# Gated linear attention and the merge in one software-pipelined loop, with the silu gate made in the projection

## The reference, cut to what matters

```python
def _gla_chunk(S, inp):            # o_t = q_t S_t, S_t = diag(alpha_t) S_{t-1} + k_t^T v_t
    b = jnp.cumsum(g, axis=1)
    o_inter = jnp.einsum('blhk,bhkv->blhv', qf * jnp.exp(b), S)
    A = jnp.einsum('bthk,bshk,btshk->bhts', qf, kf, decay)       # decay = exp(b_t - b_s), s <= t
    o_intra = jnp.einsum('bhts,bshv->bthv', A, vf)
    S_new = jnp.exp(b_last)[..., None] * S + jnp.einsum('blhk,blhv->bhkv', k_dec, vf)

def _merge(fox_o, gla_o, gr, gla_norm_g, w_out):
    gn = gla_o * lax.rsqrt(jnp.mean(jnp.square(gla_o), axis=-1, keepdims=True) + EPS)
    gated = gn.reshape(B, T, GLA_VW) * gla_norm_g * jax.nn.silu(gr)
    return jnp.concatenate([fox_o, gated], axis=-1) @ w_out
# x = x + merge; h = rmsnorm(x) * norm2_g; then the FFN on h
```

## Time and profile before

| | |
|---|---|
| median of three runs | 3477.89 us |
| the profiled execution | 3477.98 us, span 3476.2 us |
| PE busy over the span | 3133.6 us (90%) |
| DVE / ACT / POOL busy | 2027.8 / 1207.3 / 556.0 us |
| stretch of `gla` and `merge` up to the first FFN matmul | 1300.4 to 1898.4, 598.0 us |

### The profile page before, as it was taken

The page is one execution under the profiler, slowest core; times in us unless marked ns, Lnnn a source line. Parts: engine busy times, 40 slices in busy tenths (PEclk is TensorE's granted clock), DMA queues, the critical chain, the costliest instruction groups (busy, mean ns, idle before and its releaser), DMA issues. The chain is left out here.

```text
span 3476.2 us, 50599 instructions
## 1 busy us (share of the span) xinstructions
PE 3133.6 (90%) x19097; PEld 2887.6 (83%) x19097; DVE 2027.8 (58%) x3535; ACT 1207.3 (35%) x2345; POOL 556.0 (16%) x388
## 2 busy tenths in 40 slices
PE   7999999789999584665996999999999899999996
PEld 5899999768777363554775999999999899999996
DVE  5232211179999347993442666666666666666665
ACT  6352111168888224552221222222223422222223
POOL 0010000000000004650000222121222322122122
PEclk9999999889999795777998999999999999999998
DMA  4245322352431522223556211111114321111112
GB/s 119 71 150 174 129 74 56 79 104 64 90 67 32 144 119 64 79 74 114 165 165 226 71 49 42 48 45 45 48 42 162 108 79 43 48 48 42 48 33 77
DMA packets 247867, 298.79 MB, mean 86 GB/s; under 512 B 35785, under 2 KB 205062, under 8 KB 238680
## 3 DMA queue, kind: packets, MB, share of 16 engines
q1 hardware_dynamic: 245136, 289.88, 28.4%
q10 hardware_dynamic: 1344, 4.36, 0.6%
q0 software_dynamic: 1264, 2.88, 0.3%
HBM read 204.85 MB, written 92.21 MB: 85 GB/s over the span
## 5 line engine op out<-in xcount | busy, mean ns | idle before, releaser
L2290 PE MATMUL ps_ffn<-h,wsp_n 128*128 128x312 f32 (+1 forms) x6336 | 1051.8, 322 | 22.0 <-DMA h<-h2T 22.0
L2290 PEld LDWEIGHTS ps_ffn<-h,wsp_n 128*128 128x128 f32 x6336 | 1012.3, 188 | 27.1 <-issue 22.3
L2216 DVE TENSOR_TENSOR yacc<-ps_ffn,yacc 128x312 f32<-128x312 f32 (+1 forms) x1008 | 488.0, 519 | 388.3 <-PE ps_ffn L2308 388.3
L629 PE MATMUL ps_project<-hT,wsp 128*128 128x416 f32 (+1 forms) x3000 | 600.7, 356 | 0.0
L629 PEld LDWEIGHTS ps_project<-hT,wsp 128*128 128x128 f32 (+1 forms) x3000 | 546.2, 185 | 23.9 <-issue 8.7
L2308 PE MATMUL ps_ffn<-aT,dsp 128*128 128x312 f32 (+1 forms) x3168 | 547.3, 322 | 3.0 <-DVE yacc L2216 2.9
L2308 PEld LDWEIGHTS ps_ffn<-aT,dsp 128*128 128x128 f32 x3168 | 508.3, 188 | 6.6 <-DVE yacc L2216 3.5
L2192 ACT ACTIVATE aT<-a 128x416 fp32r<-128x416 f32 x132 | 65.1, 493 | 820.5 <-DVE a L2267 820.5
L2095 POOL TENSOR_TENSOR wsp_n<-wraw_n,wsp_n 128x1024 fp32r<-128x1024 f32 x88 | 210.7, 2396 | 814.8 <-ACT wsp_n L2136 814.8
L2258 DVE RECIPROCAL silu<-silu 128x416 f32<-128x416 f32 x132 | 304.9, 2310 | 28.7 <-ACT silu L2181 28.6
L485 DVE COPY zr<-ps_project 104x512 f32<-104x512 f32 x80 | 55.2, 692 | 300.6 <-PE ps_project L641 175.6
(11 more groups left out here) (261 smaller groups left out, 3544.4 us busy)
## 6 DMA issues: line engine op xcount, KB each, us to landing
wraw_n<-in_w_gate_dram SPq DMA_DIRECT2D x44, 512.0 KB, 3.8
wraw_n<-in_w_up_dram SPq DMA_DIRECT2D x44, 512.0 KB, 3.8
draw<-in_w_down_dram SPq DMA_DIRECT2D x44, 512.0 KB, 3.6
h2T<-hT_m SPq DMA_DIRECT2D x20, 832.0 KB
h<-h2T SPq DMA_DIRECT2D x20, 832.0 KB, 13.8
zT<-zs SPq DMA_DIRECT2D x12, 1040.0 KB, 4.0
wraw<-in_w_in_dram SPq DMA_DIRECT2D x24, 512.0 KB
x<-x2s SPq DMA_DIRECT2D x20, 416.0 KB
```

The costliest lines, as they stand in the source:

```text
L629: last = pe.matmul(ps[0:w, p % NB, 0:BLK], wsp[:, b, s, k, 0:w], hT[:, g * TPB:(g + 1) * TPB, v, k, :], start=k == 0 and m == 0, stop=k == ...
L2216: dve.tensor_tensor(y, z, y, ALU.add).then_inc(added, 1)
L2290: last = pe.matmul(ps[:, 2 * q + s, 0:FB[b] * TT], wsp[:, par, s, w, k, :], h2[:, FB0[b]:FB0[b + 1], v, k, :], start=m == 0, stop=m == 3 * ...
```

## The change

`gla` and `merge` become one stage `gla_merge` with a loop of steps t = 0 ... 18 over 17 chunks (chunk 0 is the 32 sample tokens, chunks 1 to 16 have 128 prompt tokens). Step t holds the scores, outputs and state of chunk t, the turning, splitting and output product of chunk t-1, and the turning of the normalised rows of chunk t-2. GLA outputs stay on chip; `mixg` and `gsq` are gone. `w_out` is loaded through a double buffer at the stage's start. The diagonal of the scores is now an elementwise product on POOL (`dq`) summed by one-column matmuls. `h2T` is laid out over all tokens instead of by tile. The gate is made in `project`, for the last four column tiles: ACT Exp and +1, DVE reciprocal and a product with the block and the norm weight.

```diff
 # project, ACT, in place of the copy L382 for n >= 21
+                if n >= N_GATE:
+                    m = p - place(N_GATE, 0)
...
+                    act.activation(silu, ps[:, p % NB, 0:BLK], ACT.Exp, scale=-1.0).then_inc(s_exp, 1)
+                    act.wait_ge(s_exp, m + 1)
+                    act.activation(silu, silu, ACT.Identity, bias=ones[:]).then_inc(s_one, 1)
+                    return
 # project, DVE
+            def gate_rows(p):
+                n, g = BLOCKS[p]
...
+                dve.wait_ge(s_one, m + 1)
+                dve.reciprocal(silu, silu).then_inc(s_inv, 1)
...
+                dve.scalar_tensor_tensor(out=zs[:, n % 2, g * BLK:(g + 1) * BLK], in0=ps[:, p % NB, 0:BLK], scalar=gn[:, n - N_GATE:n - N_GATE + 1],
+                                         in1=silu, op0=ALU.mult, op1=ALU.mult).then_inc(block_out, 1)
...
+                if N_GATE <= n < NWT:
+                    gate_rows(p)
 # gla_merge, ACT
+            for t in range(NCH + 2):
+                if is_gla(t - 1):
+                    high_m(t - 1, 0)
+                if t + 1 < NCH:
+                    exps(t + 1)
...
+                if is_gla(t):
+                    key_rows(t)
+                if t >= 2:
+                    high_h(t - 2, 0)
+                if is_gla(t - 1):
+                    high_m(t - 1, 1)
+                if t >= 2:
+                    high_h(t - 2, 1)
+                if is_gla(t):
+                    squares(t)
+                if is_gla(t - 1):
+                    square_x(t - 1)
+                if t <= NCH:
+                    roots(t)
+                if is_gla(t):
+                    scale_o(t)
 # gla_merge, DVE, the loop's body for a full step
+                    low_m(t - 1, 0)
...
+                        pick(t, i)
+                        if i == 0 and t >= 2:
+                            low_h(t - 2, 0)
+                        if i == 1 and t >= 1:
+                            low_m(t - 1, 1)
+                        if i == 5 and t >= 2:
+                            low_h(t - 2, 1)
+                    pick_diagonal(t)
...
+                    add(t - 1, 0)
...
+                    decayed(t + 1)
...
+                    add(t - 1, 1)
...
+                    update(t)
...
+                    exponents(t + 2)
...
+                    invert(t)
...
+                    norm(t - 1)
...
+                    gate(t)
 # layout of the normalised rows for the FFN
-    "x2": ((NTOK, D), F32), "h2T": ((NT, P, 2, KD, TT), F32),
+    "x2": ((NTOK, D), F32), "h2T": ((P, 2, KD, NTOK), F32),
```

More of the change, by code:

```diff
@@ L1510, in _ @@
         @block.tensor
         def _(pe):
-            pe.wait_ge(filled, 3 + 2 * NL)
-            pe.wait_ge(zeroed, 4)
-            def back(t, b, L):
-                pe.wait_ge(k_ready, t + 2)
-                pe.wait_ge(q_ready, t + 2)
-                if not isinstance(t, int) or t >= 0:
-                    pe.wait_ge(picked, (t + 1))
-                    pe.wait_ge(kd_out, t + 1)
-                for l, half in levels(L):
+            pe.wait_ge(filled, 4 + 2 * NL)
+            pe.wait_ge(zeroed, 6)
@@ L1522, in back, with scores @@
+            def scores(c):
+                b, L = c % 2, width(c)
+                pe.wait_ge(k_ready, c + 1)
+                pe.wait_ge(q_ready, c + 1)
+                if c:
+                    pe.wait_ge(picked, c)
+                if c >= 2:
+                    pe.wait_ge(added, 2 * (c - 1))
+                for l, half in levels(c):
                     for g in range(2):
@@ new lines, in _ @@
+            lows, highs = range(4), range(4, KD)
+            for t in range(NCH + 2):
+                if is_gla(t - 1):
+                    turn_mix(t - 1, 0)
+                if is_gla(t):
+                    scores(t)
+                if t >= 2:
+                    turn_h(t - 2, 0)
+                if is_gla(t - 1):
+                    turn_mix(t - 1, 1)
+                    products(t - 1, 0, lows)
+                if t >= 2:
+                    turn_h(t - 2, 1)
+                if is_gla(t - 1):
+                    products(t - 1, 0, highs)
+                if is_gla(t):
+                    outputs(t)
+                if is_gla(t - 1):
+                    products(t - 1, 1, lows)
+                    products(t - 1, 1, highs)
+                if is_gla(t):
+                    state(t)
@@ new lines, in gate @@
+            def gate(c):
+                b, L = c % 2, width(c)
+                dve.wait_ge(o_out, c + 1)
+                dve.wait_ge(v_come[b], 32 * (c // 2 + 1))
+                if c >= 2:
+                    dve.wait_ge(m_turned, 2 * (c - 1))
+                dve.tensor_tensor(mix[0:L, b, FOX:D], ov[0:L], sg[0:L, b], ALU.mult).then_inc(gated, 1)
+            exponents(0)
+            decayed(0)
+            for k in range(4):
+                low_w(k)
+            dve.wait_ge(st_in, 16)
@@ L2364, in stream_step @@
     fox_sample(nc, d)
-    gla(nc, d)
-    merge(nc, d)
+    gla_merge(nc, d)
     ffn(nc, d)
```

843 lines of the change are left out of this document (431 added, 412 removed).

## The result

The changed kernel takes 3361.26 us (median of 4 runs, 3358.64 to 3361.88) against 3478.44 for the kernel before beside it: a ratio of 0.9662, with 0.9645 to 0.9679 as the 95% interval. The forecast was 3374, the range 3345 to 3425. The profiled execution took 3358.64 us with a span of 3356.9.

A forecast was written before the change was run, and what follows sets the result against it. DVE bounded `gla` and TensorE `merge`, taking turns. Merged: 39.6 + 375 + 20.6 + 18.7 + 6.3 + 23.5 = 483.7 against 598.0 us; 3478.0 - 114.3 + 10 for the gate = 3373.7, say 3374 us, range 3345 to 3425.

The forecast's parts named there:

- What sets the step: Merged loop: ACT's queue from 0.7 to 11.35 us, DVE's picks to 17.1, then TensorE's last 7.6.
- The length of the step: Merged loop: a full step takes 25.0 us, fifteen of them 375 us.
- the walk: Merged loop: one full step followed instruction by instruction over the engines with estimated handoffs, giving 24.7 us.
- The ends: Merged stage outside the fifteen full steps: 39.6 us start, then 20.6, 18.7, 6.3 and 23.5 us.
- T = 0: Point where TensorE ends a product and DVE can add it; first full step's put 39.6 us after stage start.
- the last turn: End of merged stage: add, squares, root, norm, two turns with a split between, 6.3 us.
- the way to the FFN: From the merged stage's last turn to the FFN's first matmul: old 22.0 us plus 1.5 for h2T's layout, 23.5.
- The gate: In project: 2 us at each of three tile borders and 4 at the end, 10 us more; bounds 4 and 25.
- (2): Merged loop: ACT's queue longer through handoffs or dearer table switches, 2.8 us a step, 42 in all, 3416 us; chance 0.18.
- (3): Merged loop: TensorE binds and a step falls to 22 us, 45 us less, 3329 us; chance 0.08.
- (5): Layout change or gate costs more than set, at the bounds 6 and 25 us together, 3394 us; chance 0.17.
- (4): Merged loop: TensorE's clock falls after gaps ahead of the outputs, 7.3 us a step, 110 in all, 3484 us; chance 0.04.

The follow-up runs named there:

- e3_exps_late: Changed kernel with ScalarE's exponentials of the next chunk moved behind the high halves of the norm and of h: 3343.17 us, ratio 0.9613.
- e5_no_root: Changed kernel with the square root in the merged loop left out, so no table loads there: 3344.86 us, ratio 0.9624.
- e2_rows_first: Changed kernel with VectorE in project taking the earlier block's rows out of PSUM ahead of the newest block's gate: 3360.14 us.
- f4_late_filler_tanh: Changed kernel with exponentials behind the high halves, five unused TensorE products per full step, and project's gate made from tanh without the reciprocal: 3316.73 us, ratio 0.9538.
- f2_late_filler: Changed kernel with ScalarE's exponentials behind the high halves and five unused TensorE products added per full step: 3330.45 us.
- e8_gap: Changed kernel with seven added VectorE products ahead of each step's last pick, so TensorE stands still before the outputs: 3474.71 us.
- f1_filler_alone: Changed kernel with only five unused TensorE products added per full step, behind the scores: 3363.42 us.
- e4_invert_first: Changed kernel with VectorE's reciprocal of the roots ahead of its exponent sums: 3369.83 us, ratio 0.9688.
- e1_gate_only: Kernel before the change with only the gate moved into project, old gated attention and merge kept: 3481.8 us, ratio 1.0008.

## Why the prediction was right, point by point

**What sets the step: right.** The waits named ahead are there: VectorE 2.98 us for ScalarE's high half of h (38.7 us in 13 steps), 2.37 for TensorE ahead of the second add, TensorE 0.97 ahead of the outputs. `e3_exps_late` and `e5_no_root` show that ScalarE's queue sets it: taking the exponentials out from ahead of the high halves, or the second table load out of the queue, shortens the step. The clock in the loop is 0.97, over the 0.95 that was named.

**The length of the step: right in kind, too long by 1.4.** Predicted 25.0 (24.7 by the walk and 0.3 put on top), measured 23.58. Against the walk the high half of h ends at 10.5 instead of 10.75, the last pick at 16.2 instead of 17.1, and TensorE's last stretch takes 7.4 instead of 7.6. Of the 1.1 us of the walk, 0.25 are on ScalarE, 0.65 on VectorE between the high half and the last pick, 0.2 on TensorE. The walk added lengths where the instructions overlap: on ScalarE the exponential of 0.42 starts at 1548.58 and the next one 0.33 later, and that one, of 1.90, is followed at 1550.71, 1.80 later (rows of the step above). The Trainium skill ("ScalarE: Activation LUTs", What ACT_TABLE_LOAD costs) says that back-to-back activations overlap by some 93 ns; the trace agrees with 0.09 to 0.10. On VectorE the ten splits and picks from 1551.59 to 1557.25 have lengths that sum to 6.0 us and take 5.66, and the walk had 6.3 for them; four of the picks take 0.44 us and not the 0.52 of the earlier trace rows. TensorE's waits come out shorter too: in a step at full clock (1517.52 to 1541.09) 3.0 us in five waits of at most 1.0, not about 5 in five of at most 1.6. So this term of the sum was mis-sized, 15 x 1.4 = 21 us: nothing should have been put on top, and starts should have been subtracted, not lengths added.

**The ends: right in the sum, within 1.3 us each.** T = 0 came 38.3 us after the stage's start (39.6 predicted); the sixteenth step took 20.8 (20.6), the seventeenth 19.1 (18.7), the last turn 7.5 (6.3), the way to the FFN 23.0 (23.5). That these errors cancel (-1.3 + 0.2 + 0.4 + 1.2 - 0.5 = 0.0) is luck. The 322 GB/s that the prediction names there stand as 317 in the earlier trace rows; its 1.5 us hang little on it.

**The gate: right place, 4.4 us too cheap.** 14.4 instead of 10, with TensorE's waits at the tile borders and at the end, as said. Within it the shares were off: the copies that open a tile cost 5.5 us of waits and 1.5 of clock instead of 6, the end 7.0 instead of 4. What I missed is that the chain (4.76 us) is nearly as long as a block with its turn (5.00), so that what it loses at a border is still there when the matmuls end, and the last turns wait for it in full; `e2_rows_first` showed it by failing and `f4_late_filler_tanh` by removing the 2.75.

**The rivals.** (2) did not come: no dearer switch. (3), TensorE binding, came only once the exponentials were moved, and then at 21.33 us, not 22 (`f2_late_filler`). (5) did not come either: the gate stayed under its bound of 25, and the way to the FFN took 23.0 us, less than the term. (4) was priced at 7.3 us a step for a full fall; a real fall ahead of the outputs costs 2.3 (`e8_gap`), since the clock is back by 1531.5 and most of the product runs at the upper level. And it does not need a gap of 5 us: behind the scores the clock falls with single waits of 0.40 and 0.76 us. The Trainium skill ("TensorE: Matmul & The Clock Gate", HAM oscillation) draws such a loop with long waits for transfers; here the trace shows falls where no single wait is longer than 0.8. In the changed kernel they cost nothing only because ScalarE was later still (`f1_filler_alone`).

**The sum.** 3373.7 - 21.1 (stage) + 4.4 (gate) + 2.6 (FFN) - 0.9 (softmax attention) = 3358.7, the profiled execution. So the total was nearer than its largest term: the step came 21 us under, the gate and the FFN 7 us over. The 2.6 of the FFN stays open: from its first matmul the end comes after 1577.8 us before, 1579.1 in the gate-only kernel and 1579.4 to 1583.9 in the other eleven, with TensorE busy 1534.5 now and 1535.8 before; so it is not TensorE's work, and some of it may be scatter. It was not looked into.

## What to carry to other kernels

When two stages are laid into one loop, write out each engine's queue by start-to-start times and find which single queue the other engines wait for: here ScalarE's, and moving one call in it gave 18 us. When that wait is gone, look at the granted clock just behind the stretch where TensorE has only small matmuls and short waits: a fall that cost nothing behind another wait becomes the step, and a few matmuls of no use, put where the engine waits anyway, give it back. A chain through one buffer that is nearly as long as the block it should hide behind (here 4.76 us of 5.00) cannot make up what it loses once: shorten the chain (another form of the function) before changing its order.

## What the runs showed of the hardware that I had not expected

TensorE's granted clock went from 1.00 to 0.50 (from 1475.5 to 1477.5 in `e3_exps_late`) behind a stretch in which the engine was busy 1.45 of 2.60 us, with no wait over 0.8 us, in every second step of that kernel. It did so in every step of another, `e4_invert_first`, where it was busy 1.43 of 3.90, and in none of fourteen steps with five matmuls of 0.25 us added there. Why only every second step falls is open.

VectorE and GpSimd lengthen each other's instructions, and not evenly. A GpSimd subtraction of 128x128 takes 0.40 us where it meets neither kx nor qx (seven of them 2.56 us in the changed kernel, beside picks and splits). In the old loop and with the late exponentials seven take 6.4 to 6.7 us, because two of the seven last as long as the kx and the qx beside them. From `e3_exps_late`, the two long ones and VectorE's products:

```profile
1461.41 2.38 DVE L1839 TENSOR_TENSOR kx<-kr,ex 128x2048 f32<-128x2048 f32 x1 [0.76 <-ACT ex L1586]
1461.61 2.45 POOL L1548 TENSOR_TENSOR ex<-bs 128x128 f32<-128x128 f32 x1
...
1463.72 2.22 DVE L1841 TENSOR_TENSOR qx<-qr,ex 128x1792 f32<-128x1792 f32 x1
1464.02 2.18 POOL L1548 TENSOR_TENSOR ex<-bs 128x128 f32<-128x128 f32 x1
```

It works the other way too: qx takes 2.02 us alone (`e1_gate_only`), 2.22 beside the subtractions, and 2.56 in the changed kernel, where GpSimd's dq of 1.09 us has started ahead of it (1465.25 against 1465.66). The Trainium skill ("SBUF — State Buffer", SBUF: two separate sides) describes a port pair that the two share and that one holds for a whole instruction; the trace agrees in that each long subtraction ends 0.3 us after the product it started beside. With the late exponentials it costs nothing that shows: with the fillers TensorE is busy 99% of that loop.
